# Feeding the first projection of each norm in one pass: matmuls that wait for the low half, and a vector loop that interleaves both halves

## The reference

```python
for l in range(DEPTH):                                   # DEPTH = 2
    h = rmsnorm(x, norm1_g[l]) * (1.0 + sc1) + sh1
    proj = h @ w_in[l]                                   # attention, convolution, SSM input "su", gates
    ...
    x = x + g1 * (mixed @ w_out[l])
    h2 = rmsnorm(x, norm2_g[l]) * (1.0 + sc2) + sh2
    gu = h2 @ w_ffn_in[l]                                # SwiGLU: f_gate, f_up
    f_gate, f_up = jnp.split(gu, 2, axis=-1)
    x = x + g2 * ((jax.nn.silu(f_gate) * f_up) @ w_ffn_out[l])
return rmsnorm(x, final_norm_g)
```

## Time and profile before

| | |
|---|---|
| runs | 1015.86, 1019.4 and 1020.73 us, median 1019.4 us |
| profiled execution | 1019.4 us, of which the span is 1017.6 us |
| mean granted TensorE clock over the span | 0.971 of full |
| PE busy | 942.3 us (93%) |
| DVE busy | 669.6 us (66%) |
| ACT busy | 467.2 us (46%) |

### The profile page before, as it was taken

How to read it: one execution, slowest core, us unless ns; L and a number is a source line. 1 busy time by engine, 2 the same in 40 slices (tenths; PEclk the granted TensorE clock), 3 DMA queues, 4 the chain that set the end, 5 groups by cost and what they waited for, 6 DMA issues and landing times.

```text
span 1017.6 us, 16134 instructions
## 1 busy us (share of the span) xinstructions
PE 942.3 (93%) x6863; PEld 788.9 (78%) x6863; DVE 669.6 (66%) x913; ACT 467.2 (46%) x548; POOL 8.7 (1%) x11
## 2 busy tenths in 40 slices
PE   4788998999999999999997998999999999999995
PEld 1587975666766889898996997666676799999994
DVE  3783978899477484466447576799966664444445
ACT  4484135623745365545335323564364453434342
POOL 2000000000000000000000000000000000000000
PEclk9799999999999999999998999999999999999998
DMA  9965235548667366566658434455867635565521
GB/s 346 227 209 208 84 126 206 207 140 293 260 246 188 138 208 207 206 207 208 208 173 196 130 115 175 148 208 185 243 253 262 214 125 201 172 200 173 199 91 41
DMA packets 128023, 194.01 MB, mean 191 GB/s; under 512 B 30706, under 2 KB 90618, under 8 KB 121808
## 3 DMA queue, kind: packets, MB, share of 16 engines
q1 hardware_dynamic: 127608, 192.85, 56.6%
q10 hardware_dynamic: 344, 0.14, 0.1%
HBM read 191.93 MB, written 1.05 MB: 190 GB/s over the span
## 4 chain that ended last, share of the span: by engine, by line
PE 64%; DVE 23%; DMA 5%; ACT 4%; issue 3%; ACTq 1%; DVEq 0%
PE bank L547 18%; PE bank L549 17%; PE bank L548 17%; DVE wlo L1367 7%; DVE yc L1650 7%; PE bank L583 2%; DMA prod<-in_conv_dw_w 2%; PE bank L804 2%; PE bank L648 2%; PE bank L671 1%; ACT whi L1022 1%; DMA raw<-in_w_out 1%; DMA raw<-in_w_in 1%; PE bank L659 1%; DMA raw<-in_w_mod 1%
## 5 line engine op out<-in xcount | busy, mean ns | idle before, releaser
L1367 DVE TENSOR_TENSOR wlo<-raw,whi 128x2048 fp32r<-128x2048 f32 (+1 forms) x135 | 302.7, 2243 | 237.4 <-PE bank L549 185.5
L1022 ACT ACTIVATE whi<-raw 128x2048 fp32r<-128x2048 f32 x132 | 252.3, 1912 | 159.7 <-DMA raw<-in_w_in 76.1
L547 PE MATMUL bank<-hhi,whi 128*128 128x256 f32 x928 | 267.1, 288 | 2.5 <-DVE wlo L1367 2.5
L548 PE MATMUL bank<-hlo,whi 128*128 128x256 f32 x928 | 264.0, 284 | 0.0
L549 PE MATMUL bank<-hhi,wlo 128*128 128x256 f32 x928 | 263.9, 284 | 0.0
L547 PEld LDWEIGHTS bank<-hhi,whi 128*128 128x128 f32 x928 | 179.4, 193 | 10.6 <-issue 5.9
L548 PEld LDWEIGHTS bank<-hlo,whi 128*128 128x128 f32 x928 | 179.4, 193 | 0.6
L549 PEld LDWEIGHTS bank<-hhi,wlo 128*128 128x128 f32 x928 | 179.4, 193 | 0.0
L547 PE MATMUL bank<-whi,bhi 128*128 128x512 f32 x304 | 122.6, 403 | 3.4 <-DVE wlo L1367 3.4
L548 PE MATMUL bank<-wlo,bhi 128*128 128x512 f32 x304 | 120.2, 395 | 0.0
L549 PE MATMUL bank<-whi,blo 128*128 128x512 f32 x304 | 120.0, 395 | 0.0
(11 more groups left out here) (256 smaller groups left out, 908.5 us busy)
## 6 DMA issues: line engine op xcount, KB each, us to landing
raw<-in_w_mod SPq DMA_DIRECT2D x48, 1024.0 KB, 7.2
raw<-in_w_ffn_in SPq DMA_DIRECT2D x44, 1024.0 KB, 5.2
raw<-in_w_in SPq DMA_DIRECT2D x38, 1024.0 KB, 5.5
raw<-in_w_ffn_out SPq DMA_DIRECT2D x22, 1024.0 KB, 5.0
raw<-in_w_out SPq DMA_DIRECT2D x8, 1024.0 KB, 6.8
raw<-in_w_in SPq DMA_DIRECT2D x16, 256.0 KB, 5.0
raw<-in_ssm_glu_b SPq DMA_DIRECT2D x4, 1024.0 KB, 5.1
raw<-in_ssm_glu_a SPq DMA_DIRECT2D x4, 1024.0 KB, 5.1
```

What stands on the lines that cost most here:

```text
L547: mm(o, w_hi, a_hi, start=start, stop=False, skip_group_check=True)
L548: mm(o, w_hi, a_lo, start=False, stop=False, skip_group_check=True)
L1022: fn(whi[mi % N_HI][:, :], raw[SLOT[item]][:, :], ACT.Copy).then_inc(s_hi, 1)
L1367: part = V.tensor_tensor(wlo[mi % N_LO][:, n], raw[SLOT[("main", *divmod(mi, NB))]][:, n], whi[mi % N_HI][:, n].bitcast(F32), ALU.subtract)
```

## The change

In PE's `main_block` the two passes of the first block behind a norm become one pass. For each k PE waits for hlo_ready (which is later than hhi_ready, so the wait for hhi_ready is dropped), and issues all six matmuls of that k through `hi_lo`, for c = 0 and c = 1. The number and the shapes of the matmuls stay the same.

In DVE's `norm` the two loops become one of ten turns: turn k makes h[k] (while k is below 8) and then hlo[k - 2] (from k = 2 on). The order is h0, h1, h2, lo0, h3, lo1, ... h7, lo5, lo6, lo7. Instructions and waits stay the same in number. ACT's code is not touched.

```diff
                 if n == 0 and kind in ("su", "fg"):
 
                     o = unit_bank(l, i)
-                    h0 = H_PER_LAYER * l + H0[kind]
                     for k in range(DK):
-                        pe.wait_ge(hhi_ready, h0 + k + 1)
+                        done = H_PER_LAYER * l + H0[kind] + k + 1
+                        pe.wait_ge(hlo_ready, done)
                         for c in range(2):
-                            for w in w8:
-                                mm(o[:, c * T:(c + 1) * T], w[:, k, c * P:(c + 1) * P], hhi[:, k, :], start=(k == 0 and c == 0 and w is w8[0]), stop=False,
-                                   skip_group_check=True)
-                    for k in range(DK):
-                        pe.wait_ge(hlo_ready, h0 + k + 1)
-                        for c in range(2):
-                            last = mm(o[:, c * T:(c + 1) * T], w8[0][:, k, c * P:(c + 1) * P], hlo[:, k, :], start=False, stop=(k == DK - 1),
-                                      skip_group_check=True)
+
+                            last = hi_lo(o[:, c * T:(c + 1) * T], w8[0][:, k, c * P:(c + 1) * P], w8[1][:, k, c * P:(c + 1) * P], hhi[:, k, :], hlo[:, k, :],
+                                         k == 0 and c == 0, k == DK - 1)
                     last.then_inc(s_unit, 1)
...
-                for k in range(DK):
-                    V.scalar_tensor_tensor(out=h[:, k, :], in0=turned_x(n, k), scalar=s[:, k:k + 1], in1=rinv_rows[:, :],
-                                           op0=ALU.mult, op1=ALU.mult).then_inc(h_full, 1)
-                for k in range(DK):
-                    dve.wait_ge(hhi_ready, h0 + k + 1)
-                    V.scalar_tensor_tensor(out=hlo[:, k, :], in0=h[:, k, :], scalar=modv[:, shift + k:shift + k + 1],
-                                           in1=hhi[:, k, :].bitcast(F32), op0=ALU.add, op1=ALU.subtract).then_inc(hlo_ready, 1)
+                for k in range(DK + 2):
+                    if k < DK:
+                        V.scalar_tensor_tensor(out=h[:, k, :], in0=turned_x(n, k), scalar=s[:, k:k + 1], in1=rinv_rows[:, :],
+                                               op0=ALU.mult, op1=ALU.mult).then_inc(h_full, 1)
+                    if k >= 2:
+                        j = k - 2
+                        dve.wait_ge(hhi_ready, h0 + j + 1)
+                        V.scalar_tensor_tensor(out=hlo[:, j, :], in0=h[:, j, :], scalar=modv[:, shift + j:shift + j + 1],
+                                               in1=hhi[:, j, :].bitcast(F32), op0=ALU.add, op1=ALU.subtract).then_inc(hlo_ready, 1)
```

## The result

The changed kernel takes 1025.28 us (median of 14 runs, 1021.88 to 1029.57) against 1020.6 us for the kernel before (14 runs, 1015.86 to 1022.26). The ratio is 1.0052 with a 95% interval of 1.0037 to 1.0066, so the change costs 3.8 to 6.7 us, not the 2.0 us of the forecast; 1025.28 lies inside the range of 1017.2 to 1025.9. The profiled execution of the changed kernel took 1024.41 us with a span of 1022.6.

The account below looks back on a forecast made before the run. PE, and the DVE work it waits for, were taken to bound the kernel. Terms 0.3 + 0.64 + 0.37 + 0.64 = +1.95, about +2.0 us on 1019.4, gave 1021.4 us; range 1017.2 to 1025.9, forecast chance 0.55.

Parts of the forecast that it names:

- The start: PE's first matmul behind a norm waits for lo0 instead of hhi0: +0.62 us at norm 1, 0.64 used.
- DVE's order: DVE's interleaved h and lo pieces: no wait added at norms 1 to 3; 0.28 us before lo4 at norm 0, charged +0.3.
- ACT and supply: ACT's later hhi pieces cost nothing, 1.7 us of cover left; at half clock PE never waits again for low halves.
- The low bound of a block at full clock: PE's block at full clock throughout is held to DVE's pace: +0.3 to +0.4 us.
- What the delay costs: PE's 0.64 us later start costs 0.64 at norm 1, 0.37 at norm 2, 0.64 at norm 3; norm 0 +0.3 over DVE.
- the first, more stretches at half clock: PE's longer gap brings extra half-clock stretches, 1.5 us each: 1022.9 with one, 1024.4 two, 1027.4 four; chance 0.18.
- Rival 2: PE's waits between groups keep half clock through the whole block: +13.6 us, 1033.0; chance 0.03.
- Rivals 3 to 5: Half-clock stretches avoided, 1018.4 or 1016.9, chance 0.13; ACT becomes the bound, 1024.0, 0.03; nothing arrives, 1019.4, 0.08.
- The base: Starting time of the sum: the profiled execution before, 1019.4 us, taken as also the median of the runs.

Follow-up runs that it names:

- 12 fillers: Changed kernel plus 12 extra matmuls of 256 columns in PE's gap before each of the four blocks: 1023.16 against 1020.14 us for the kernel before, ratio 1.0037.
- DVE's loop: Kernel before with only DVE's interleaved loop, PE keeping its two passes: 1021.39 us against 1020.68, ratio 1.0008 (0.9997 to 1.0019).
- the pass with waits that starts at hhi0: Changed kernel, but PE's one pass issues four matmuls of hhi[k], then two of hlo[k-2]: 1021.95 us against 1020.14 for the kernel before, ratio 1.0008.

## Why the prediction was wrong

**The start.** Right in size: predicted 0.62 to 0.64 us, measured 0.66 at norm 0, 0.64 at norm 1 (the gap of 1.69 became 2.33).

**DVE's order.** Right at norms 1 to 3, no wait was added. At norm 0 the wait in front of lo4 was 0.41 us against 0.28 predicted, and the weight subtraction came 0.52 later against 0.28: hhi3 began late as well, since it waited 0.26 us for h3, and pushed ACT's weight copy and hhi4 (42.82 instead of 42.59) back by 0.23 us. That wait I had left out. (In the steady order a low half starts 1.5 us behind the end of its h, not 1.2 as I wrote; that makes the cover larger.)

**ACT and supply.** Right at norms 1 to 3: the subtraction behind each of these blocks still waits for PE. At norm 0 ACT is on the path, with the copy in front of hhi4. At half clock PE waited for no low half. The low bound of a block at full clock was wrong: I let the last six matmuls follow lo7, but from lo5 on, PE is behind and not DVE. The block of the changed kernel with 12 fillers, at full clock, ends 335.67 - 327.77 = 7.9 us behind h0, the one of before 1.17 + 5.83 = 7.0: +0.9, not +0.3 to +0.4. So the 0.9 that I gave as the lower end for three norms is the cost at one where the clock is full throughout.

**The step that failed** is "What the delay costs". I charged 0.64, 0.37 and 0.64 for PE's start at norms 1 to 3, nothing for it at norm 0 and 0.3 for DVE there, 1.95 in all, with an upper bound of 4 x 0.64 = 2.6. The whole change cost 3.8 to 6.7 us: above my upper bound. Three terms of the sum were too small. First, PE's start: 1.65 us charged, while starts that came 2.8, 6.1 and 10.4 us later in sum cost 3.2, 7.0 (both beyond DVE's loop) and 9 us, about 1 us per us. The changed kernel's 2.6 us are then worth 2.3 to 2.9, by the middle values. So neither the discount at norm 2 nor the nothing at norm 0 holds. Second, DVE's loop: 0.3 charged, 0.8 measured (0 to 2). Third, the clock: I left it out of the sum, taking it that it would rise at the same moments and that a block would stay 7.2 to 7.6 us long. Two of the four blocks left these bounds, norm 2 with 8.46 and norm 3 with 7.87. In all three profiles of the changed kernel the block of norm 2 is 8.39 to 8.47 us long, but in the second profile of before it is 8.51; what the change does to it is open. Changed alone, norm 0 gave +1.8 us (0 to 3.7). (At norms 1 to 3 alone the measured 1.6, -0.2 to 3.4, is no evidence against my 1.65.) The profile of norm 0 alone shows DVE 0.77 us later behind norm 0, of which 0.28 us were there before its first h, and nothing more that differs beyond the scatter of the clock.

**The rival that came in part** is the first, more stretches at half clock, which I gave 0.18. The first profile has three more, two of which reach into blocks. By its own price (2.0 + 1.5 each) two to three stretches give 1022.9 + 1.5 to 1022.9 + 3.0, 1024.4 to 1025.9, and measured were 1025.28; that the forecast plus this price meets the measured time is partly luck, since the base was 1.2 us low and the terms of the forecast were too small. Over runs: the half-clock time was 72.6 us on average in 20 runs of the changed kernel (mean clock 0.9646, mean span 1023.3) and 64.4 in 100 timed runs of before (0.9684, 1018.4). The 8.2 us more are 2.4 stretches. But not all of them are work at half the pace, part is the longer gap itself. In the profiles the stretches, added up from windows of 0.5 us, sum to 61.9 and 59.0 us before, with PE busy in 43.5 and 41.3 of them, and to 72.4, 72.3 and 73.3 changed, with PE busy in 49.5, 49.1 and 48.1. On average that is 12 us more at half clock, 6.5 of it with PE busy; at half the pace these are worth an estimated 3 us. The kernels with filler, where less half clock brought so little, speak against taking such a price at its word. I argued against this rival that all four blocks had their stretch already; a block can have more than one, and one profile of before shows that it also may have none.

**Rival 2**, half clock through the whole block, did not come: the longest block of the changed kernel is 8.5 us where 10.2 would be needed, and the pass with waits that starts at hhi0 costs nothing measurable. What the Trainium skill says in "TensorE: Matmul & The Clock Gate", section "Loop structure matters more than you think", is that a long wait for a load in front of every matmul sends the clock down; my prediction left out the word "long". The waits between groups here are too short to test it: with 12 fillers the groups come 0.79 us apart with 0.72 us of work in each, and the clock stayed at full through these blocks. **Rivals 3 to 5** did not come. To avoid stretches on purpose, by filling the gap, was tried and brought no gain.

**The base.** The profiled execution of before, at 1019.4 us, was 1.2 us below the median of the 14 runs (1020.6). My sum stood on it, and that is part of why 1021.4 missed 1025.28.

**What stays open.** The direct delay of 0.64 us at norms 1 to 3 (1.9), 0.35 us per block at these three (1.05, an indication only) and DVE's 0.5 at norm 0 make 3.5 of the 4.7 to 5.3 us. The remaining 1.2 to 1.8 us may lie in where the clock's steps fall outside the blocks (DVE's weight subtraction that stands at 114.08 us in the first profile of before comes 1.7 to 3.5 us later in the three of the changed kernel, but 4.0 us later in the second profile of before, too), in norm 0, and in the single pass. The runs don't separate these.

## What to carry to other kernels

When a consumer is the bound, the moment when it can start is worth more than the tidiness of its loop: matmuls that need only the high half should go out while the low half is made. A delay in front of a dense block costs its own length, here about 1 us per us in three experiments; don't discount it for a stretch at half clock. Measure the delay that a control really makes: a second wait behind the first added 0.1 us at three of four norms. One profile fixes neither the base nor the clock: before building a sum on it, look how far it lies from the median of the runs, and profile the same kernel again before a difference between two profiles is read as an effect.

## What the runs showed of the hardware

- The same block of 48 matmuls took 5.83, 7.3 and 8.5 us in profiles of one kernel, by where the granted clock stepped between 1.2 and 2.4 GHz. At norm 1 an idle gap of 1.69 us was followed by a fall 0.7 us into the block in one profile of before, and by none in the other.
- Extra matmuls in the gap raise the mean clock (0.968 to 0.973 with 6 per norm) without a faster kernel (0.9997, 0.9981 to 1.0014).
- PE stood still for 3.0 us up to 475 us on nothing that the profile shows, in one kernel with 32 more matmuls, and ran at half clock behind it. Every profile has such a wait of 1.7 to 3.0 us in front of the matmuls of L648.
- Six matmuls of 128 x 128 by 256 columns go out every 0.79 us when their low half comes at that pace, at full clock, and the clock stayed at full.
